# Narrow TensorE products issued as pairs of 64 weight columns, and another order in the first steps of a recurrence

## The reference

```python
n_cmp = (S - CMP_LEN) // CMP_STRIDE + 1          # 15
def compress(k, pos, w1, w2):
    blocks = k[:, :, cidx, :] + pos
    flat = blocks.reshape(B, G, n_cmp, CMP_LEN * Dh)   # 2048 long
    return jax.nn.gelu(flat @ w1) @ w2                 # w1: 2048 x 256
```

```python
def step(state, inp):
    sa = jnp.einsum('bhvk,bhk->bhv', state, -kk_t)
    state = (state * w_t[:, :, None, :] + sa[..., None] * (kk_t * a_t)[:, :, None, :]
             + v_t[..., None] * k_t[:, :, None, :])
    y = jnp.einsum('bhvk,bhk->bhv', state, r_t)
```

## Time and profile before

| | |
|---|---|
| median of 3 runs | 2143.38 us (2141.55 to 2144.43) |
| profiled execution, its own time | 2146.24 us |
| its span in the trace | 2144.4 us |
| mean granted TensorE clock | 0.991 |
| TensorE (PE) busy | 2068.1 us, 96% |
| weight loads (PEld) busy | 1927.5 us, 90% |
| VectorE (DVE) / ScalarE (ACT) busy | 1340.8 us, 63% / 1002.3 us, 47% |
| DMA engines | 44.3% of 16 engines' span |

### The profile page before, as it was taken

How to read it: one execution, slowest core, us unless ns; L and a number is a source line. 1 busy time by engine, 2 the same in 40 slices (tenths; PEclk the granted TensorE clock), 3 DMA queues, 4 the chain that set the end, 5 groups by cost and what they waited for, 6 DMA issues and landing times. The chain is left out here.

```text
span 2144.4 us, 40380 instructions
## 1 busy us (share of the span) xinstructions
PE 2068.1 (96%) x16930; PEld 1927.5 (90%) x16930; DVE 1340.8 (63%) x1985; ACT 1002.3 (47%) x1433; POOL 13.0 (1%) x12
## 2 busy tenths in 40 slices
PE   7999999999999999999999989999999989999998
PEld 7999987999999998799989979989998988998997
DVE  6555565754655456575557666577776846577776
ACT  5343356433543335554335444455546534456543
POOL 0000000000000000000000010000000010000000
PEclk9999999999999999999999999999999989999999
DMA  8534531554454362265344324366434423346551
GB/s 312 212 144 145 207 118 71 227 201 157 174 233 176 128 223 80 74 243 204 137 178 161 109 95 139 100 237 245 178 146 157 149 75 101 128 138 261 202 196 50
DMA packets 79872, 348.84 MB, mean 163 GB/s; under 512 B 21232, under 2 KB 30576, under 8 KB 45808
## 3 DMA queue, kind: packets, MB, share of 16 engines
q1 hardware_dynamic: 79728, 346.74, 44.3%
HBM read 345.67 MB, written 1.05 MB: 162 GB/s over the span
## 5 line engine op out<-in xcount | busy, mean ns | idle before, releaser
L89 PE MATMUL bank<-ffn_hT_split,n_split_gate_up 128*128 128x256 f32 x1408 | 392.8, 279 | 2.8 <-DVE ffn_hT_split L192 2.4
L90 PE MATMUL bank<-ffn_hT_split,n_split_gate_up 128*128 128x256 f32 x1408 | 392.2, 279 | 0.0
L91 PE MATMUL bank<-ffn_hT_split,n_split_gate_up 128*128 128x256 f32 x1408 | 392.1, 279 | 0.0
L89 PEld LDWEIGHTS bank<-ffn_hT_split,n_split_gate_up 128*128 128x128 f32 x1408 | 265.6, 189 | 5.2 <-issue 3.7
L90 PEld LDWEIGHTS bank<-ffn_hT_split,n_split_gate_up 128*128 128x128 f32 x1408 | 265.8, 189 | 1.5
L91 PEld LDWEIGHTS bank<-ffn_hT_split,n_split_gate_up 128*128 128x128 f32 x1408 | 266.9, 190 | 0.0
L356 ACT ACTIVATE work<-bank 128x256 f32<-128x256 f32 x88 | 33.3, 383 | 315.2 <-PE bank L91 315.2
L1801 DVE TENSOR_TENSOR mix_parts<-mix_arrived,mix_parts 128x1024 fp32r<-128x1024 f32 x88 | 107.6, 1223 | 96.4 <-ACT mix_parts L1796 96.2
L455 DVE TENSOR_TENSOR work<-bank,work 128x256 f32<-128x256 f32 x88 | 37.2, 423 | 194.1 <-ACT work L356 194.1
L436 DVE TENSOR_TENSOR ffn_split_down<-ffn_arrived_down,ffn_split_down 128x2048 fp32r<-128x2048 f32 x44 | 100.8, 2291 | 81.2 <-ACT ffn_split_down L351 81.2
L419 DVE TENSOR_TENSOR n_split_gate_up<-arrived_gate_up,n_split_gate_up 128x2048 fp32r<-128x2048 f32 x64 | 144.4, 2287 | 9.5 <-ACT n_split_gate_up L341 9.5
(11 more groups left out here) (392 smaller groups left out, 5828.5 us busy)
## 6 DMA issues: line engine op xcount, KB each, us to landing
arrived_gate_up<-in_ffn SPq DMA_DIRECT2D x64, 1024.0 KB, 8.5
ffn_arrived_down<-in_ffn SPq DMA_DIRECT2D x44, 1024.0 KB, 4.8
mix_arrived<-in_mix_w SPq DMA_DIRECT2D x88, 512.0 KB, 3.5
rrived_gate_up<-in_conv_ffn SPq DMA_DIRECT2D x32, 1024.0 KB, 6.7
_arrived_gate_up<-in_ffn SPq DMA_DIRECT2D x24, 1024.0 KB, 6.6
mixer_arrived<-in_w_in SPq DMA_DIRECT2D x22, 1024.0 KB, 7.2
onv_ffn_arrived_down<-in_conv_ffn SPq DMA_DIRECT2D x22, 1024.0 KB, 4.8
irst_project_arrived<-in_w_in SPq DMA_DIRECT2D x17, 1024.0 KB, 5.0
```

Source lines behind the costliest of these rows:

```text
L89: pe.matmul(out, lhs[0], rhs[0], start=start, stop=False)
L90: pe.matmul(out, lhs[0], rhs[1], start=False, stop=False)
L91: return pe.matmul(out, lhs[1], rhs[0], start=False, stop=stop)
```

## The change

1. `matmul_halves` issues a product of 128 weight columns as two products of 64 weight columns, into the lower and the upper 64 partitions of the same bank, with the same moving operand. It is used in `hidden_columns` and in the six groups of the recurrence's outputs.
2. The low-rank products alternate between rows 0 to 63 and rows 64 to 127.
3. In the scan, pieces 2 and 3 are placed anew: piece 2 leaves its place before the steps and goes into step 0, behind `turn_branch(2)`; piece 3 goes from step 0 to step 1, ahead of `turn_branch(3)`; `spatial(1)` goes behind `outer_product(0)`. ScalarE's and VectorE's `after(2)` and `after(3)` move along, and VectorE's `gate_units(1)` goes behind its addition of step 0.

```diff
+def matmul_halves(pe, out, lhs, rhs, **kind):
+    for rows in (slice(0, DH), slice(DH, P)):
+        last = pe.matmul(out[rows], lhs[:, rows], rhs, **kind)
+    return last
...
             for j in range(CJ):
-                last = pe.matmul(out, c.wc1[:, v, j, f * P:(f + 1) * P], c.kcols[:, v, :, j, :],
-                                 start=(j == 0), stop=(j == CJ - 1))
+                last = matmul_halves(pe, out, c.wc1[:, v, j, f * P:(f + 1) * P], c.kcols[:, v, :, j, :],
+                                     start=(j == 0), stop=(j == CJ - 1))
...
-        for half, first_bank in ((0, 4), (1, 6)):
-            rows = slice(half * DH, (half + 1) * DH)
-            for j in range(PAIRS):
+        for j in range(PAIRS):
+            for half, first_bank in ((0, 4), (1, 6)):
+                rows = slice(half * DH, (half + 1) * DH)
                 last = pe.matmul(c.ps[first_bank + j // 2][:, (j % 2) * S:(j % 2 + 1) * S],
                                  c.low_rank[rows, j * P:(j + 1) * P], c.thin[rows, 0, :], start=True, stop=True)
...
-    AT_STEP = {0: (3,), **{n: (2 * n, 2 * n + 1) for n in range(2, TOTAL)}}
+    AT_STEP = {0: (2,), 1: (3,), **{n: (2 * n, 2 * n + 1) for n in range(2, TOTAL)}}
...
                            c.ps[2 + e][DH:P].rearrange("p (c n) -> p c n", c=NT), ACT.Copy).then_inc(s["cross_copied"], 1)
-        after(2)
         copy_inverse(0)
...
         keep(1, 3)
-        after(2)
...
                 branch_low(2 + n)
-            if n == 0:
-                gate_units(1)
             for m in AT_STEP.get(n, ()):
                 after(m)
             for h in range(2):
...
                 dve.tensor_tensor(part, part, bank_units(4 + h)[:, 0:4], ALU.add).then_inc(s["updated"], 1)
+            if n == 0:
+                gate_units(1)
...
         score(1, 2)
-        piece(2)
         pe.wait_ge(s["cross_copied"], 2)
...
-            last = pe.matmul(c.ps[4][:, head_cols(u)], pairs_of[:, u, P:2 * P], c.vt[:, 0, head_cols(u)],
-                             start=True, stop=True, skip_group_check=True)
+            last = matmul_halves(pe, c.ps[4][:, head_cols(u)], pairs_of[:, u, P:2 * P], c.vt[:, 0, head_cols(u)],
+                                 start=True, stop=True, skip_group_check=True)
...
-            if n < 2:
-                turn_branch(2 + n)
+            if n == 0:
+                turn_branch(2)
+            for m in AT_STEP.get(n, ()):
+                piece(m)
+            if n == 1:
+                turn_branch(3)
+            outer_product(n)
             if n == 0:
                 spatial(1)
-            for m in AT_STEP.get(n, ()):
-                piece(m)
-            outer_product(n)
```

More of the change, by code:

```diff
@@ L2091, in tensor @@
         pe.wait_ge(s["low_loaded"], 48)
-        for half, first_bank in ((0, 4), (1, 6)):
-            rows = slice(half * DH, (half + 1) * DH)
-            for j in range(PAIRS):
+        for j in range(PAIRS):
+            for half, first_bank in ((0, 4), (1, 6)):
+                rows = slice(half * DH, (half + 1) * DH)
                 last = pe.matmul(c.ps[first_bank + j // 2][:, (j % 2) * S:(j % 2 + 1) * S],
                                  c.low_rank[rows, j * P:(j + 1) * P], c.thin[rows, 0, :], start=True, stop=True)
-            last.then_inc(s["small_ready"], 1)
+                if j == PAIRS - 1:
+                    last.then_inc(s["small_ready"], 1)
         project(8, N_RW)
@@ L2934, in tensor @@
         for u in range(NH):
[L2935 to L2938, removed]
+            matmul_halves(pe, c.ps[4][:, head_cols(u)], pairs_of[:, u, 0:P], w_rows[0][:, head_cols(u)],
+                          start=True, stop=False, skip_group_check=True)
+            last = matmul_halves(pe, c.ps[4][:, head_cols(u)], pairs_of[:, u, 2 * P:3 * P], c.vt[:, 0, head_cols(u)],
+                                 start=False, stop=True, skip_group_check=True)
         last.then_inc(s["y_ready"], 1)
         for u in range(NH, 2 * NH):
-            pe.matmul(c.ps[7][:, head_cols(u)], pairs_of[:, u, P:2 * P], c.vt[:, 1, head_cols(u)],
-                      start=(u == NH), stop=False, skip_group_check=True)
+            matmul_halves(pe, c.ps[7][:, head_cols(u)], pairs_of[:, u, P:2 * P], c.vt[:, 1, head_cols(u)],
+                          start=(u == NH), stop=False, skip_group_check=True)
         for u in range(NH, 2 * NH):
-            pe.matmul(c.ps[5][:, head_cols(u)], pairs_of[:, u, 2 * P:3 * P], c.vt[:, 1, head_cols(u)],
-                      start=(u == NH), stop=False, skip_group_check=True)
+            matmul_halves(pe, c.ps[5][:, head_cols(u)], pairs_of[:, u, 2 * P:3 * P], c.vt[:, 1, head_cols(u)],
+                          start=(u == NH), stop=False, skip_group_check=True)
         piece(TAIL)
@@ L2962, in tensor @@
         for u in range(NH, 2 * NH):
-            last = pe.matmul(c.ps[5][:, head_cols(u)], pairs_of[:, u, 0:P], w_rows[1][:, head_cols(u)],
-                             start=False, stop=True, skip_group_check=True)
+            last = matmul_halves(pe, c.ps[5][:, head_cols(u)], pairs_of[:, u, 0:P], w_rows[1][:, head_cols(u)],
+                                 start=False, stop=True, skip_group_check=True)
         last.then_inc(s["y_ready"], 1)
```

## The result

The changed kernel takes **2106.52 us** (median of 4 runs, 2101.04 to 2107.16), the kernel before beside it 2143.41 (2141.55 to 2144.43): ratio **0.9823**, 95% interval 0.9805 to 0.9841. That is 36.9 us by the medians, 1.8% by the ratio. By the profiled executions it is 2146.24 to 2107.12, 39.1 us. Five more runs on another chip had a median of 2106.31, ratio 0.979 (0.9763 to 0.9817).

The account below looks back on a forecast made before the run. TensorE, busy 96% of the span, was taken as the bound, with weight loads setting narrow passes' distance. Terms 11.0 + 3.0 - 0.9 + 6.2 + 1.9 + 11.0 = 32.2 us gave 2111 us, range 2101 to 2128.

Parts of the forecast that it names:

- Compression groups: Compression's 8 groups: 32 pairs at 0.058 us replace 32 passes at 0.112; 1.72 saved less 0.34 each, 11.0 us.
- rival (a): Column halves do not run side by side, 0.116 us a pair; 6.4 us gained in all, 2137 us; chance 0.12.
- the excursion: Entering and leaving the divided array around a list of half products, costed at 0.34 us each time.
- Clock behind the first groups: Clock stretches at 0.50 behind each layer's first compression group go, about 1.5 us each, 3.0 us in all.
- Late swap: The swap after compression comes earlier and now waits about 0.45 us for its read; minus 0.9 us for both layers.
- Outputs: Recurrence outputs, lines 2935 to 2944: 64 passes a layer go from 7.15 to 3.72 us; 6.2 us in all.
- which eats most of what 2830 saves: Scan's first steps: transposes behind line 2830 wait some 0.4 us, cancelling most of that list's 0.5 us saving.
- Low-rank: Low-rank products: alternating row halves take 1.92 us where they took 2.89; 0.97 a layer, 1.9 us in all.
- First steps: Scan's first steps: moved pieces cover TensorE's waits, piece 4 starts 5.5 us earlier a layer; 11.0 us for both.
- the weakest term, the clock: Scan's first stage: stretches at clock 0.50 may go or come twice; 5 us either way.
- (b): First steps' reorder gives only line 2830's share because another wait takes its place; 10 us less gain, 2121; chance 0.11.
- (c): Every change between column halves makes TensorE wait, 0.09 us for 448 half products; 40 us slower, 2177; chance 0.05.

Follow-up runs that it names:

- f3_quarters: The changed kernel with all compression products issued as four quarters of 32 weight columns instead of two halves of 64; 2107.99 us, ratio 0.9806.
- g1_middle_quarters: The changed kernel with quarters of 32 weight columns in each layer's second and third compression groups, halves in the first and fourth; 2108.97 us, ratio 0.9821.
- g2_output_quarters: The kernel with quarters in the second and third compression groups, plus the four output lists behind the scan as quarters too; 2115.97 us, ratio 0.9839.
- e3_low_rank: The kernel before with only the low-rank products' two row halves alternating; 2142.59 us, ratio 0.9984.

## Why the prediction was right, step by step

2111 was forecast with 2101 to 2128; 2106.5 came. By the profiled executions, 32.2 us were forecast and 39.1 measured. By the table of stages, compression gave 13.45 (13.1 forecast), low-rank 1.94 (1.9), the scan's part 21.46 (17.2), and the rest of the program 2.2, where nothing was forecast.

- **Compression groups**: 0.058 us a pair was right, and rival (a) is out. It had the sentence of the Trainium skill (TensorE: Matmul & The Clock Gate, Part 3, "What overlaps and what doesn't") that a weight load runs beside products in flight only where the row group differs; this trace differs, since these halves use all 128 rows and a pair starts every 0.058 us. Both other sizes of the step were off, and by luck they cancel: the group of before is 3.49 us, not 3.58, and the excursion is 0.13 (0.31 instead of 0.22 ahead of the first pass, 0.04 behind the last), not 0.34. Per group 3.49 - 1.98 - 0.09 = 1.42 where 1.38 was forecast.
- **Clock behind the first groups**, 3.0: the stretches are gone, but the reason given (groups half as long) is not shown: the low-rank kernel lacked one with whole groups, and the unpaired halves, whose groups last 3.64 us, lacked both. Here the time was right without the reason.
- **Late swap**, -0.9: waits of 0.56 and 0.41 came. The compression stages together lost 6.63 + 6.82 = 13.45 us, forecast 13.1.
- **Outputs**, 6.2: the list of 2935 to 2944 gives 3.2 a layer, as summed. The step that failed is "which eats most of what 2830 saves": in the changed kernel the list of line 2830 and the transposes behind it take 2.32 us (1247.68 to 1250.00) where they took 2.81, so all of its 0.49 stays. The transposes do not wait in the first layer and wait 0.15 us in the second, and the last scores wait 0.21 where 0.4 was forecast. Line 2963 gives nothing, as said.
- **Low-rank**: 1.92 us a layer forecast, 1.92 measured.
- **First steps**: `turn_branch(2)` to piece 4 was to be 11 us; 1250.62 to 1261.50 is 10.88. Alone, 5.67 for 5.5.
- **What was mis-sized is the weakest term, the clock.** Its direction was left open, "5 us either way", and that it came as a gain is luck by the prediction's own account. In the profiles the second layer's scan part lost 12.7 us where the first lost 8.7, and the second is the one that had the 13.65 us stretch. That a few idle microseconds start such a stretch is not shown: f3_quarters has none behind an idle 2.62 us, g1_middle_quarters has one behind 2.03. Over 53 and 9 executions the changed kernel keeps a clock 0.006 higher. At 1.5 us for 0.001 that is some 9 us, of which the forecast had 6.0 (3.0 behind the first groups, 1.5 in each layer's first steps). The 3 us that are left are the greater part of the 4.7 that the sum lacks to the first comparison's 36.9, by this estimate; the second surprise of the last section is a rival for them, and two sets of four runs can't divide them.

Rivals (b) and (c) fell: no new wait over 0.6 us in the first steps, and no price for a change between halves.

## What to carry to other kernels

Where many products in a row move few columns, TensorE's time is the weight load's: issue them as column halves that alternate, where many stand together (lists of 16 passes paid here, places of 2 and 4 did not), and look at the moving columns, and at how fast the code can come, before going smaller. Read a part's worth from its own stage in the trace when executions of one program spread by 16 us, and take the mean granted clock beside every time. Before costing a gain ahead of a wait, follow the chain that ends the wait; if it starts earlier than your edit, count nothing.

## What the runs showed that was not expected

- Column halves over all 128 rows run side by side, and so do column quarters (four passes in 0.033 us with 30 moving columns), until TensorE stands still for up to 2.8 us with no releaser but "issue" and goes on 1.25 to 1.49 us after a 16 KB packet of the instruction queue has ended.
- At a granted clock of 1.00, the same passes come at one of two distances for long stretches. Windows of the kernel before from the first to the last start of 96 passes with 256 columns in the feed-forward part:

```profile
438.14:449.33 11.19, 11.19 (x97) 11.19 (x95) 4.84 (x5) 2.31 (x2) 0.00 (x0) 1.00 0.48 187
611.74:622.53 10.79, 10.79 (x96) 10.79 (x95) 4.86 (x5) 2.32 (x2) 0.00 (x0) 1.00 0.48 181
```

  11.19 / 95 = 0.118 us and 10.79 / 95 = 0.114, with the same DMA share. Of 10662 distances between passes with 256 columns, before has 3842 at the longer value (116 to 122 ns), the changed kernel 3184: 658 x 0.0042 = 2.8 us of the 39.1 between the profiles. The other kernels here had 2872 to 4158, in no order that follows the edits, but g2_output_quarters 6810. Its profiled execution took 2131.26 us at a clock of 0.994, and the other four of the same kernel 2111 to 2117; the 3626 longer distances more than the changed kernel's are 15 us by the same sum. What sets it stayed open, and it is a part of what two executions differ by at the same clock.
- The stretch from compression to compression of the two mixers, which no edit touches, took 498.8 us before and 494.3 after: 1390 longer distances against 395, 4.2 us of the 4.5. e3_low_rank has 494.3 too, with 411.
